# Dealing each expert's token slots over the partitions in steps of four, and another order for the last sums

## The reference

```python
h = x + merged @ lw['w_o']
hn = rmsnorm(h, lw['norm2']).reshape(bsz * seq, D_MODEL)
h = h + hier_moe(hn, ...)            # top-1 of 4 groups, then top-2 of its 8 experts
y = rmsnorm(h, lw['norm_f'])
# inside hier_moe, for each expert e and its tokens xb:
return (jax.nn.silu(xb @ w1[e]) * (xb @ w3[e])) @ w2[e]
```

## Time and profile before

| | us |
|---|---|
| median of 3 runs | 1201.05 |
| lowest, highest | 1200.89, 1204.86 |
| the profiled execution | 1199.92 |
| its span, first to last instruction | 1198.3 |
| TensorE busy | 1085.6 (91%) |
| VectorE busy | 356.5 (30%) |
| ScalarE busy | 230.0 (19%) |
| GpSimd busy | 133.4 (11%) |

### The profile page before, as it was taken

How to read it: one execution, slowest core, us unless ns; L and a number is a source line. 1 busy time by engine, 2 the same in 40 slices (tenths; PEclk the granted TensorE clock), 3 DMA queues, 4 the chain that set the end, 5 groups by cost and what they waited for, 6 DMA issues and landing times.

```text
span 1198.3 us, 16684 instructions
## 1 busy us (share of the span) xinstructions
PE 1085.6 (91%) x6911; PEld 778.1 (65%) x6911; DVE 356.5 (30%) x766; ACT 230.0 (19%) x442; POOL 133.4 (11%) x151
## 2 busy tenths in 40 slices
PE   7999999999999999999999879997787787888876
PEld 6888888897888888878855445544444444444442
DVE  3994306923233142221544431010000000000003
ACT  4103021135222222250022211111111111101103
POOL 2113310002100100000000011111111111011000
PEclk9999999999999999999999979999899999998899
DMA  6771266324656654377447389999999999999983
GB/s 226 252 256 55 106 211 244 123 94 152 237 187 212 215 184 175 138 246 294 169 170 289 127 348 399 417 415 420 416 419 420 423 421 420 421 422 420 419 354 126
DMA packets 48858, 330.76 MB, mean 276 GB/s; under 512 B 8811, under 2 KB 11963, under 8 KB 35344
## 3 DMA queue, kind: packets, MB, share of 16 engines
q1 hardware_dynamic: 31744, 257.65, 53.5%
q0 software_dynamic: 15024, 64.31, 15.5%
q10 hardware_dynamic: 2016, 7.76, 1.6%
HBM read 319.77 MB, written 61.85 MB: 318 GB/s over the span
## 4 chain that ended last, share of the span: by engine, by line
PE 66%; DMA 29%; ACT 2%; DVE 1%; issue 1%; SPq 0%; ACTq 0%; DVEq 0%; POOLq 0%
DMA arena<-in_w 25%; PE bank L864 14%; PE bank L687 14%; PE bank L1186 8%; PE bank L1049 5%; PE bank L1211 5%; PE bank L1040 4%; PE bank L779 2%; PE bank L960 2%; DMA arena<-in_w_stream 2%; PE bank L700 1%; PE bank L853 1%; PE bank L879 1%; PE bank L900 1%; ACT arena L1463 1%; PE bank L888 1%
## 5 line engine op out<-in xcount | busy, mean ns | idle before, releaser
L1186 PE MATMUL bank<-arena 128*64 128x256 f32 x2048 | 260.8, 411 | 68.2 <-DMA arena<-in_w 67.5
L1186 PEld LDWEIGHTS bank<-arena 128*64 128x64 f32 x2048 | 159.1, 143 | 161.7 <-issue 56.0
L864 PE MATMUL bank<-arena 128*128 128x260 f32 x768 | 173.1, 384 | 0.0
L687 PE MATMUL bank<-arena 128*128 128x260 f32 x768 | 170.1, 383 | 0.3 <-DMA arena<-in_w_stream 0.2
L687 PEld LDWEIGHTS bank<-arena 128*128 128x128 f32 x768 | 145.4, 190 | 23.4 <-DMA arena<-in_w_stream 0.7
L864 PEld LDWEIGHTS bank<-arena 128*128 128x128 f32 x768 | 144.1, 190 | 22.4 <-issue 1.2
L1211 PE MATMUL bank<-arena 128*64 128x512 f32 x512 | 115.5, 593 | 4.1 <-DVE arena L2050 2.5
L2044 DVE TENSOR_TENSOR arena<-arena,bank 128x256 f32<-128x256 f32 x32 | 13.5, 422 | 323.0 <-ACT arena L1520 323.0
L643 POOL DMA_INDIRECT y_dram<-arena,scatter_rows x30 | 42.9, 1430 | 372.7 <-ACT arena L1533 338.6
L1211 PEld LDWEIGHTS bank<-arena 128*64 128x64 f32 x512 | 36.8, 136 | 64.6 <-issue 56.8
L1520 ACT ACTIVATE arena<-bank 128x256 f32<-128x256 f32 x32 | 12.3, 385 | 322.4 <-PE bank L1186 322.4
(11 more groups left out here) (340 smaller groups left out, 1085.3 us busy)
## 6 DMA issues: line engine op xcount, KB each, us to landing
arena<-in_w SPq DMA_DIRECT2D x95, 2048.0 KB, 36.0
arena<-in_w_stream SPq DMA_DIRECT2D x56, 512.0 KB, 3.5
out_sample_swa_k<-in_cache_swa_k POOLq DMA_DIRECT2D x8, 2047.0 KB, 10.3
out_sample_swa_v<-in_cache_swa_v POOLq DMA_DIRECT2D x8, 2047.0 KB, 10.4
arena<-in_cache_mem_v SPq DMA_DIRECT2D x8, 512.0 KB, 6.1
arena<-in_w_o SPq DMA_DIRECT2D x2, 2048.0 KB, 14.8
out_sample_swa_k<-in_cache_swa_k POOLq DMA_DIRECT2D x8, 511.0 KB, 6.2
out_sample_swa_v<-in_cache_swa_v POOLq DMA_DIRECT2D x8, 511.0 KB, 6.0
```

The source lines that it names most:

```text
L687: last = pe.matmul(bank[:, 2 * u + h, 0:HALF], ring[u][:, k, :], x[:, k, h * HALF:(h + 1) * HALF], start=k == 0, stop=k == KT - 1)
L864: last = pe.matmul(bank[:, h, 0:HALF], ring[n % 2][:, k, :], xn[:, k, h * HALF:(h + 1) * HALF], start=k == 0, stop=k == KT - 1)
L1186: last = pe.matmul(bank[64 * q:64 * q + CAP, 2 + u, part * FE // 2:(part + 1) * FE // 2], xgT[e // 2 % 2][:, k, 64 * u:64 * u + CAP], w[:, ...
```

## The change

**Slots.** `place` now compares the rank with the slot numbers in another layout: column 4a + b of `hot` is set by rank 16b + a, with a from 0 to 15 and b from 0 to 3. Ranks 0, 1, 2, ... so go to partitions 0, 4, 8, ..., 60, then 1, 5, 9, ..., and so on. One comparison per tile of 128 entries becomes two of 64, written with a stride of four.

**The end.** Tiles are taken in the order 0, 1, 2, 3, 4. VectorE adds tiles 0, 1, 2 and the decode tile (4), and TensorE adds only tile 3 with the identity product, directly ahead of that tile's `add_end`. The banks follow: tile 4 reuses the bank of tile 0, so its `add_end` waits until tile 0 has been added.

```diff
-END_ORDER = (4, 0, 1, 2, 3)
-END_BANK = {4: 0, 0: 2, 1: 4, 2: 6, 3: 0}
-BY_PE = (0, 1)
-BY_DVE = (4, 2, 3)
+END_BANK = (2, 4, 6, 0, 2)
+BY_PE = (3,)
+BY_DVE = (0, 1, 2, 4)
...
-            for T in END_ORDER:
+            for T in range(NT):
                 sp.dma_start(h_back[T][0:ROWS[T], :], h_acc[T * P:T * P + ROWS[T], :]
...
-            for T in BY_PE:
-                add_rows(T)
             pe.wait_ge(s["yc"], NE + 2)
             pe.wait_ge(*later("yend", 1))
-            for T in END_ORDER:
-                if T == 3:
+            for T in range(NT):
+                if T in BY_PE:
+                    add_rows(T)
+                if T == 4:
                     pe.wait_ge(*later("added", 1))
                 add_end(T)
...
+            def dealt(x):
+
+                return x.rearrange("p (a b) -> p b a", a=16)
+
+            slots = c["slot"].rearrange("p (b a) -> p b a", a=16)
...
-                TT(hot[:, i], c["slot"].unsqueeze(1).to_broadcast([P, 2, CAP]),
-                   slotk[:, i, :].unsqueeze(2).to_broadcast([P, 2, CAP]), ALU.is_equal).then_inc(s["hot"], 1)
+                for k in range(2):
+                    place = TT(dealt(hot[:, i, k, :]), slots, wide(slotk[:, i, k:k + 1], 2, (CAP // 16, 16)),
+                               ALU.is_equal)
+                place.then_inc(s["hot"], 1)
...
-            add_placed(4)
-            finish(0)
-            finish(1)
-            add_placed(2)
-            finish(2)
-            add_placed(3)
+            add_placed(0)
+            add_placed(1)
+            finish(0)
+            add_placed(2)
+            finish(1)
+            finish(2)
+            add_placed(4)
             finish(3)
             finish(4)
```

More of the change, by code:

```diff
@@ L517, in _ @@
             sp.wait_ge(s["fdone"], 1)
-            for T in END_ORDER:
+            for T in range(NT):
                 sp.dma_start(h_back[T][0:ROWS[T], :], h_acc[T * P:T * P + ROWS[T], :]
                              ).then_inc(h_back_in(T)[0], 16)
-            for i, T in enumerate(END_ORDER):
+            for i, T in enumerate(range(NT)):
                 sp.wait_ge(s["fin"], i + 1)
@@ L2014, in slot_tables_again @@
                 dve.wait_ge(s["rtab"], p * 6 - 5)
-                TT(hot, c["slot"].unsqueeze(1).unsqueeze(1).to_broadcast([P, NT, 2, CAP]),
-                   slotk.unsqueeze(3).to_broadcast([P, NT, 2, CAP]), ALU.is_equal).then_inc(s["hot"], 1)
+                for i in range(NT):
+                    for k in range(2):
+                        last = TT(dealt(hot[:, i, k, :]), slots, wide(slotk[:, i, k:k + 1], 2, (CAP // 16, 16)),
+                                  ALU.is_equal)
+                last.then_inc(s["hot"], 1)
                 for k in range(2):
@@ L2097, in add_placed @@
                 dve.wait_ge(*h_back_in(T))
-                dve.wait_ge(*later("sums", END_ORDER.index(T) + 1))
+                dve.wait_ge(*later("sums", T + 1))
                 TT(h_back[T][0:n], h_back[T][0:n],
@@ L2103, in finish @@
             def finish(i):
-                T = END_ORDER[i]
+                T = i
                 n = ROWS[T]
```

## The result

Over 13 runs of each, the changed kernel takes 1205.59 us (median) and the kernel before 1200.31: a ratio of 1.004, 95% interval 1.0026 to 1.0054, so 3.1 to 6.5 us slower. The forecast was 1205.0.

A forecast was written before the change was run, and what follows sets the result against it. The fullest DMA engine was taken to bound the last stretch. Dealing +7.0, first gather -0.4 and end -2.7 made +3.9 us: 1203.8 profiled, 1205.0 median; own range 1201 to 1210, with rivals 1193 to 1212.

The forecast's parts named there:

- What bounds the kernel: Last stretch, while weights stream in: the DMA engine with the most work sets the time; TensorE has slack.
- The sum for one engine: Fullest DMA engine from SP's second half load on: 436 us of weights, 39.9 us of gathered and scattered rows.
- Which engine serves which slot: Scatter: slots 2k, 2k+1, 32+2k and 33+2k on engine k; gather: four neighbours in each block of 32.
- both rivals that rested on another assignment: Scatter slots: four neighbours share an engine, 1193.6 us, chance 0.14; every sixteenth slot shares one, 1211.5 us, chance 0.08.
- The third, that the skew costs nothing: DMA engines: those still working go faster when others idle, leaving only the end's gain; 1198 us, chance 0.06.
- Dealing the slots, 7.0 us: Gathers and scatters beside the weights: even engines get more scattered rows, so the latest engine ends 7.0 us later.
- The sum of rows alone: Gathered and scattered rows on the fullest engine: 46.0 us after dealing against 39.9 before, 6.1 us later.
- The allowance for this in the prediction, 0.9 us: Dealing term: 7.0 taken over 6.1, as eight engines lie within 5 us and the latest catches extra work.
- The first gather, 0.4 us won: Before SP's second half load: 6 rows instead of 8 on the fullest engine; 0.4 us won, between 0 and 1.5.
- The end, 2.7 us won: After the last `down`: fewer identity products on TensorE, VectorE becomes the one to follow; 2.7 us won.
- VectorE's schedule: At the end: additions of tiles 0 and 1 end at 1180.4 and 1182.3; decode tile finished at 1192.5.
- The sum: Whole kernel: 7.0 - 0.4 - 2.7 = +3.9 us, giving 1203.8 profiled and 1205.0 as the median.

The follow-up runs named there:

- gather_only: Kernel before with every slot out of bounds for the scatters alone; 1181.68 us in one execution, beside 1201.04 for before.
- steps of two: Slots dealt with rank 32b + a at partition 2a + b, with the end of before, against the kernel before; 0.9963, 4.4 us faster.
- steps of eight: Slots dealt in steps of eight, with the end of before, against the kernel before; 1.0178, 21 us slower.
- slots4: The change's dealt slots alone, with the end of before, against the kernel before; 1.0076, 9.1 us slower.
- no_rows: Kernel before with every slot out of bounds for gathers and scatters; 1170.72 us in one execution, beside 1201.04 for before.
- end: The change's new end alone, with the slots of before, against the kernel before; 0.9981, 2.3 us faster.
- turn_end: Undealt slots, filled from the other end for every second pair of experts, with the new end, against the kernel before; 0.9917, 10 us faster.
- the best way of dealing: Slots dealt in steps of two, with the new end, against the kernel before; 0.9929, 8.5 us faster.

## Why the prediction was right

Point by point:

- **What bounds the kernel** was right. In all but two of the kernels the last `down` begins 0.1 us after the last landing of weights; in the profiled execution of the changed kernel TensorE's slow `up` made it 1.7, and in `gather_only` 0.5. The sum for one engine, 436 + 39.9 against a streaming time of 474.8, came out better than its parts: it left out the 4 us of empty slots and fetches above, and it took packet times that add up to 1.01 of the time, 4.7 us too many over 475. In differences between kernels both nearly drop out.
- **Which engine serves which slot** was right: pairs in the scatter, fours in the gather. The half share for 20 us, the signs of steps of two and of eight, and the groups of eight, four and four engines with steps of eight say so; both rivals that rested on another assignment are out. The third, that the skew costs nothing, fell with `slots4`.
- **Dealing the slots, 7.0 us** had the right mechanism and was somewhat too small: 8.7 and, in `slots4`, 7.6 by the streaming time, 9.1 (7.2 to 11.2) by the times of `slots4`. The sum of rows alone said 6.1. Against that sum every kernel but that with steps of two comes out later:

| kernel | fullest engine by the sum, us | from before | streaming time, us | from before |
|---|---|---|---|---|
| before | 39.9 | | 474.8 | |
| steps of two | 34.5 | -5.4 | 469.5 | -5.3 |
| every second pair turned | 30.3 | -9.6 | 468.0 | -6.8 |
| steps of four (whole change, alone) | 46.0 | +6.1 | 483.5, 482.4 | +8.7, +7.6 |
| steps of eight | 55.1 | +15.2 | 492.6 | +17.8 |

  Steps of four, of eight and turning come out 1.5 to 2.8 us over the sum. The allowance for this in the prediction, 0.9 us, was the term that was mis-sized. Its reason, that many engines lie close together at the top and the latest catches something, is not shown: before, two engines stood out by the count (39.9 and 37.9, the next 34.3), but with steps of two five lie within 3 us and nothing came on top. `no_rows` shows that engines drift apart by up to 5 us without rows; whether the excess is that, stays open.
- **The first gather, 0.4 us won**, did not show. SP's second half load came at 697.49 before, but between 697.4 and 700.8 in all the kernels run, `end` with the old slots among them at 699.23. That start moves by more than the term; in the profile after it was 0.8 us of loss. From the first gather to that load it takes 5.31 and 5.06 us with the old slots (before, `end`) and 5.17 and 5.25 with steps of four, so there is no gain to be seen.
- **The end, 2.7 us won**, was right in size: 2.3 (1.3 to 3.4) by `end`, 3.2 in the changed kernel's profile. Part of that is luck, since two errors cancel. VectorE's schedule, which was to give all of it, gave 1.8 in `end` and 2.3 in the changed kernel; the stretch with the smaller last store, counted as nothing, gave 0.9 in both. The schedule had one step wrong: VectorE's first addition came 1.5 us after its sum. Before, VectorE idled 6.06 us there until 1182.92, which hid its branch over the second pass.
- **The sum.** 8.7 + 0.8 - 3.2 and 1.7 for the slow last `up` make 8.0, against 7.75 between the two profiled executions. Without the slow `up`, and with a usual start of the weights, it is about 5.5; the medians differ by 5.3, and the ratio says 4.8. So the forecast of 3.9 lies within the interval of 3.1 to 6.5, and by these values was 0.9 to 1.4 us too low, which the allowance and the first gather would explain. That 1205.0 stands so close to the 1205.59 measured is partly luck: it was built on a median of 1201.05 for before, which over 13 runs became 1200.31.

## What to carry to other kernels

When a stretch is bound by transfers, ask what the fullest DMA engine carries, not what all carry together: a load is there only when its last engine is done, and the shares of the last windows show how far the engines have drifted apart. Which engine serves a partition has to be found for the very transfer in question, since here 128 and 64 partitions split differently; here counting rows and empties in its first microsecond gave it, and other steps bore it out. Work that differs from step to step can also be balanced by turning the order every second time: `turn_end` was at least as fast as the best way of dealing, 0.9917 (0.9904 to 0.9929) against 0.9929 (0.9917 to 0.9942).

## What the runs showed of the hardware that was not expected

- A transfer over 64 partitions gave each DMA engine two neighbouring slots and the two 32 higher; over 128 partitions four neighbours and the four 32 higher. The Trainium skill, "DMA: Bandwidth & Descriptors", section The descriptor swizzle, gives the second; the first is what these runs show. For the second the trace agrees: with gathers alone the engines finished the last load 12.5 us apart, where the count by that split gives 10.7.
- VectorE's step over a branch that was not taken into the second pass delayed its next instruction: in the changed kernel VectorE was idle for 3.46 us, 1.5 of them after the tile's sum was there. Before, the same branch lay within a wait of 6.06 us and cost nothing.
- TensorE's granted clock near the end was 0.60 in a window after a wait of 3.07 us in the changed kernel and 0.80 after one of 2.48 in `gather_only`, but 1.00 after one of 2.75 in `slots4`. So the length of the wait alone does not tell whether the last `up` takes 3.84 us or up to 6.55.
- Without any rows to move, the sixteen engines still ended up to 5.2 us apart after 444 us.
